# Position-bias tables read from 128 stored copies instead of turned by TensorE products

## The reference, cut to what matters

```python
REL_BUCKETS = 32; REL_MAX_EXACT = 16; REL_MAX_DIST = 128
def rel_bucket(dist):
    n = jnp.maximum(dist, 0)
    is_small = n < REL_MAX_EXACT
    large = REL_MAX_EXACT + (log(n / REL_MAX_EXACT) / log(REL_MAX_DIST / REL_MAX_EXACT) * 16).astype(int32)
    return where(is_small, n, minimum(large, REL_BUCKETS - 1))
...
x = x + 0.5 * swiglu(rmsnorm(x), w_ffn1_gate, w_ffn1_up, w_ffn1_down)      # first FFN
lg = einsum(q, k) * scale + tab[head, rel_bucket(t - s)]                     # mixer scores, s > t masked
```

## Time and profile before

| | |
|---|---|
| median of 3 runs | 1628.88 us (1625.75 to 1630.94) |
| profiled execution | 1628.55 us, its span 1627.2 us |
| granted TensorE clock, mean | 0.995 of full speed |
| TensorE (PE) busy | 1596.4 us, 98% of the span |
| VectorE (DVE) busy | 1036.8 us, 64% |
| ScalarE (ACT) busy | 868.8 us, 53% |
| GpSimd (POOL) busy | 126.7 us, 8% |
| moved by SP's queue q1 | 272.40 MB |
| moved by POOL's queue q0 | 6.37 MB |

### The profile page before, as it was taken

One profiled execution on the slowest core, in us unless ns is written; L12 is line 12 of the kernel. 1 busy time (PEld: TensorE's weight loads), 2 busy tenths in 40 slices (PEclk: granted clock), 3 DMA queues, 4 the chain that ended last, 5 costly groups with the idle time before them and its releaser, 6 DMA issues. The chain is left out here.

```text
span 1627.2 us, 26648 instructions
## 1 busy us (share of the span) xinstructions
PE 1596.4 (98%) x11270; PEld 1389.9 (85%) x11270; DVE 1036.8 (64%) x1430; ACT 868.8 (53%) x1272; POOL 126.7 (8%) x117
## 2 busy tenths in 40 slices
PE   7999999999999999999998999999999999999998
PEld 7888897888888898888997888888888898888886
DVE  5656564467665766567895686657766574686655
ACT  6555544446555655555755265555655555665553
POOL 0000020000000001000376001000020001001000
PEclk9999999999999999999999999999999999999999
DMA  7754554334555555654530155554655543445552
GB/s 283 286 180 174 183 167 155 105 104 179 204 199 181 181 206 182 207 181 156 185 105 4 55 207 207 184 204 156 234 180 193 195 156 129 153 170 204 199 181 78
DMA packets 40854, 280.46 MB, mean 172 GB/s; under 512 B 4794, under 2 KB 4794, under 8 KB 8864
## 3 DMA queue, kind: packets, MB, share of 16 engines
q1 hardware_dynamic: 39024, 272.40, 48.0%
q0 software_dynamic: 1712, 6.37, 1.1%
HBM read 277.14 MB, written 1.08 MB: 171 GB/s over the span
## 5 line engine op out<-in xcount | busy, mean ns | idle before, releaser
L233 PE MATMUL P<-xt,whi 128*128 128x512 f32 (+1 forms) x3264 | 729.6, 347 | 3.0 <-ACT whi L207 1.5
L233 PEld LDWEIGHTS P<-xt,whi 128*128 128x128 f32 x3264 | 561.1, 191 | 75.1 <-issue 9.1
L221 DVE TENSOR_TENSOR wlo<-raw,whi 128x2048 fp32r<-128x2048 f32 x245 | 560.1, 2290 | 66.5 <-PE P L233 53.6
L207 ACT ACTIVATE whi<-raw 128x2048 fp32r<-128x2048 f32 x245 | 467.4, 1909 | 117.9 <-PE P L233 97.0
L233 PE MATMUL P<-xt,wlo 128*128 128x256 f32 x2544 | 440.3, 283 | 0.0
L233 PEld LDWEIGHTS P<-xt,wlo 128*128 128x128 f32 x2544 | 387.5, 191 | 17.8
L607 DVE SCALAR_TENSOR_TENSOR AR<-P,AR 128x256 f32<-128x256 f32 x228 | 96.4, 423 | 240.4 <-ACT AR L600 240.4
L233 PE MATMUL P<-whi,hh 128*128 128x512 f32 x504 | 197.9, 393 | 0.0
L233 PE MATMUL P<-wlo,hh 128*128 128x512 f32 x504 | 196.8, 390 | 0.0
L233 PE MATMUL P<-whi,hl 128*128 128x512 f32 x504 | 196.1, 389 | 0.0
L600 ACT ACTIVATE AR<-P 128x256 f32<-128x256 f32 x228 | 85.8, 376 | 138.4 <-PE P L233 138.3
(11 more groups left out here) (226 smaller groups left out, 1026.7 us busy)
## 6 DMA issues: line engine op xcount, KB each, us to landing
raw<-ws SPq DMA_DIRECT2D x249, 1024.0 KB, 4.9
gb<-gains SPq DMA_DIRECT2D x14, 512.0 KB, 7.4
AR<-by_distance POOLq DMA_DIRECT2D x1, 3072.0 KB, 19.5
x<-x_in SPq DMA_DIRECT2D x2, 512.0 KB, 4.1
AR<-mem_in POOLq DMA_DIRECT2D x1, 1024.0 KB, 5.3
AR<-gains SPq DMA_DIRECT2D x2, 512.0 KB, 4.8
out<-x SPq DMA_DIRECT2D x2, 512.0 KB, 2.6
cs<-cst SPq DMA_DIRECT2D x1, 737.0 KB, 13.4
```

The costliest lines, as they stand in the source:

```text
L207: act.e.activation(k.whi[n % NHI][:, :], k.raw[u % NRAW][:, :], ACT.Copy).then_inc(*k.s_hi.inc(u))
L221: dve.e.tensor_tensor(k.wlo[n % NLO][:, :], k.raw[u % NRAW][:, :], k.whi[n % NHI][:, :].bitcast(F32), ALU.subtract).then_inc(*k.s_lo.inc(u))
L233: return pe.e.matmul(o, l, r, start=start, stop=stop, skip_group_check=True)
```

## The change

The values by distance are stored in DRAM 128 times per head: `by_distance` becomes 16 x 128 x 512, written by one DMA whose source is the same 16 partitions, each row repeated 128 times (4 MB). With 128 copies behind one another, a partition step of 511 values walks one copy further and one value back, so a single DMA reads the rows in the right order. POOL then issues two reads in place of one: `HANK` with 8 heads x 384 values, for the compressed keys only, and `BIAS` itself with 16 heads x 256 values. The products with `FLIP`, the copies from bank 7, the `FLIP` constant and its load go away. `CB` is made by two copies in ScalarE straight from `HANK`, at j = 8 instead of j = 10. The mixer's first scores wait for the DMA of `BIAS` instead of ScalarE's last copy.

```diff
-    k.dist = nc.dram_tensor("by_distance", (16, 512), F32).ap()
+    k.dist = nc.dram_tensor("by_distance", (16, 128, 512), F32).ap()
...
-    k.HANK = ar(k, 7168, 6144, "p (h c) -> p h c", h=16)
+    k.HANK = ar(k, 7168, 3072, "p (h c) -> p h c", h=8)
...
 def bias_tensor(k, pe, j):
-    if j >= 2:
-        r = j - 2
-        pe.wait_ge(*k.s_hank.after())
-        pe.wait_ge(*k.s_flip.after())
-        if r == 0:
-            pe.wait_ge(*k.s_ev.after("dist"))
-        else:
-            pe.wait_ge(*k.s_ea.after("bias", r - 1))
-        if r < 8:
-            last = mm(pe, k.P[7][:, :], k.FLIP, k.HANK[:, 2 * r:2 * r + 2, 0:256])
-        else:
-            for a in range(2):
-                c = 159 - 128 * a
-                last = mm(pe, k.P[7][:, a * 120:(a + 1) * 120], k.FLIP, k.HANK[:, 8:16, c:c + 225:16])
-        last.then_inc(*k.s_pe.inc("bias", r))
...
 def bias_scalar(k, act, j):
-    if j >= 2:
-        r = j - 2
-        act.wait_ge(*k.s_pe.after("bias", r))
-        if r < 8:
-            act.e.activation(k.BIAS[:, 2 * r:2 * r + 2, :], k.P[7][:, :].rearrange("p (h c) -> p h c", h=2),
-                             ACT.Copy).then_inc(*k.s_ea.inc("bias", r))
-        else:
-            act.e.activation(k.CB, k.P[7][:, 0:240].rearrange("p (a h n) -> p h a n", a=2, h=8),
-                             ACT.Copy).then_inc(*k.s_ea.inc("bias", r))
+    if j == 8:
+        act.wait_ge(*k.s_hank.after())
+        for a in range(2):
+            c = 159 - 128 * a
+            act.e.activation(k.CB[:, :, a, :], k.HANK[:, :, c:c + 225:16], ACT.Copy).then_inc(*k.s_ea.inc("cb", a))
...
 def bias_pool(k, pool):
     pool.wait_ge(*k.s_ev.after("dist"))
-    pool.e.dma_start(k.dist[:, :], k.VALS).then_inc(*k.s_dist.inc(by=16))
+    pool.e.dma_start(k.dist[:, :, :], k.VALS.unsqueeze(1).to_broadcast([16, 128, 512])).then_inc(*k.s_dist.inc(by=16))
     pool.wait_ge(*k.s_dist.after())
-    pool.e.dma_start(k.HANK, bass.AP(k.dist.tensor, 0, [[1, 128], [512, 16], [1, 384]])).then_inc(*k.s_hank.inc(by=16))
+    n, m = 511, 128 * 512
+    pool.e.dma_start(k.HANK, bass.AP(k.dist.tensor, 8 * m + 127, [[n, 128], [m, 8], [1, 384]])).then_inc(*k.s_hank.inc(by=16))
+    pool.e.dma_start(k.BIAS, bass.AP(k.dist.tensor, 127, [[n, 128], [m, 16], [1, 256]])).then_inc(*k.s_bias.inc(by=16))
...
     if step == 1:
         dve.wait_ge(*k.s_pe.after("cl"))
-        dve.wait_ge(*k.s_ea.after("bias", 8))
+        dve.wait_ge(*k.s_ea.after("cb", 1))
...
-            return [k.s_dup[0].after(), k.s_dup[1].after(), k.s_po.after("dup", 0), k.s_ea.after("bias", 7)] + (
+            return [k.s_dup[0].after(), k.s_dup[1].after(), k.s_po.after("dup", 0), k.s_bias.after()] + (
...
 def mixer_pool(k, pool):
-    pool.wait_ge(*k.s_ea.after("bias", 8))
+    pool.wait_ge(*k.s_ea.after("cb", 1))
...
-    pool.e.dma_start(k.FLIP, k.cst[:, C_FLIP:C_FLIP + 128]).then_inc(*k.s_flip.inc(by=16))
```

More of the change, by code:

```diff
@@ L25 @@
 C_ID, C_TRI, C_KEEP, C_CEN, C_BLK = 0, 128, 256, 384, 512
-C_MLT, C_MLE, C_LEV, C_SCAN, C_I64, C_ONES, C_FLIP = 642, 706, 770, 1154, 1410, 1474, 1602
-C_END = C_FLIP
-C_SEL = C_FLIP + 128
+C_MLT, C_MLE, C_LEV, C_SCAN, C_I64, C_ONES, C_END = 642, 706, 770, 1154, 1410, 1474, 1602
+C_SEL = C_END
 C_ALL = C_SEL + 72 + 768
@@ L146, in tiles_and_signals @@
     k.s_gn = [sig("gn0"), sig("gn1")]
-    k.s_id, k.s_vec, k.s_cst, k.s_flip, k.s_base, k.s_rel = (
-        sig(n) for n in ("id", "vec", "cst", "flip", "base", "rel"))
-    k.s_dist, k.s_hank, k.s_w2, k.s_mem = (sig(n) for n in ("dist", "hank", "w2", "mem"))
+    k.s_id, k.s_vec, k.s_cst, k.s_base, k.s_rel = (
+        sig(n) for n in ("id", "vec", "cst", "base", "rel"))
+    k.s_dist, k.s_bias, k.s_hank, k.s_w2, k.s_mem = (sig(n) for n in ("dist", "bias", "hank", "w2", "mem"))
     k.s_dup = [sig(f"dup{i}") for i in range(8)]
@@ L939, in mixer_tiles @@
     k.VALS = k.AR[0:16, 13840:14352]
-    k.FLIP = k.AR[:, 14352:14480]
     k.QA = ar(k, 7168, 1024, "p (j t) -> p j t", j=4)
@@ L3218, in constants @@
     c[:, C_ONES:C_ONES + 128] = 1
-    c[:, C_FLIP:C_FLIP + 128] = np.eye(128)[::-1]
     for j in range(6):
```

## The result

The changed kernel takes 1640.83 us (median of 7 runs, 1638.34 to 1649.99) against 1628.88 us before (7 runs now, 1625.75 to 1632.83); the ratio is 1.0083, 95% interval 1.0054 to 1.0112. It is slower by 12 us where I forecast 8 us faster, and it lies outside my range, which ended at 1628.0 us. The profiled execution took 1639.22 us. It is rival C, the slow write that starves the weights, in its mechanism and its time; the two numbers that it was worked out from were a write of 64 us and 115 GB/s for the weights, and here they are 48.3 us and 93 GB/s.

A forecast was written before the change was run, and what follows sets the result against it. TensorE, busy 98% of the span, was taken as the bound; 8.2 us saved, with 0 for DMA traffic, gave 1628.55 - 8.2 = 1620.3 us, forecast as a 1620.6 us median, range 1618.0 to 1628.0 us.

The forecast's parts named there:

- rival C: First FFN: a 64 us write leaves the weights 115 GB/s, TensorE loses 19.7 us, time 1640 us; chance 8%.
- What bounds the kernel: First FFN: TensorE never idles, busy all 74.00 us from 106 to 180 us, so a `FLIP` product costs 0.86 us.
- The saving of 6.0 + 2.2 = 8.2 us: TensorE, first FFN: seven `FLIP` products give 6.0 us, the last products and a wait at its end 2.21 us.
- Rival A: End of first FFN: VectorE's and ScalarE's chain takes back 2.2 us, leaving 6.0 us gained, 1622.9 us; chance 15%.
- ScalarE, the waits for `HANK` and `BIAS`: First FFN and mixer: removed copies count nothing; both transfers arrive 45 us before 180 us even at worst.
- The duration of the write: POOL's queue from 47 us: the 4.19 MB write takes 30 us, from the earlier read's 161 GB/s and somewhat more.
- bounds of 17 and 64 us: Write time from the small write's row: 17 us by engine time over all 16 engines, 64 us by bytes over time.
- the reading as bytes over time: Small write's row: 33 KB in 0.5 us, 66 GB/s, which gives 64 us for the 4.19 MB write.
- So I take 0 for it: Foreign traffic's cost to TensorE in the first FFN: supply of 184 against 190 GB/s loses 1.6 us, taken by slack.
- The limit of about 10.5 us from issue to landing: Weight loads in the first FFN: landing times up to about 10.5 us do not reach TensorE.
- 5.6 us of slack: Weights' chain to TensorE: missed supply absorbed before TensorE loses time, the landing limit of 10.5 less 4.9 us undisturbed.
- The rule of the Trainium skill: DMA write: partitions 0 to 15 reach four of 16 ports, 104 GB/s, so the write would take 40 us.

The follow-up runs named there:

- e1_one_copy: Changed kernel with one stored copy of the values (32 KB) instead of 128, its tables in reverse row order: 1620.33 us, ratio 0.9939.
- e4: e1_one_copy plus a 4.19 MB scratch write to DRAM out of 128 SBUF partitions, each row 16 times: 1621.35 us, ratio 0.994.
- e5: e1_one_copy plus a 4.19 MB scratch write to DRAM out of 16 neighbouring SBUF partitions, each row 128 times: 1640.03 us, ratio 1.006.
- e7: As e5, but the 16 source partitions are 0, 8, 16, ... 120 instead of 0 to 15: 1621.56 us, one run.
- e3: Changed kernel with 24 copies (0.79 MB) instead of 128, and 24 reads, one per head and table, instead of two: 1622.45 us, ratio 0.9945.
- e6: Changed kernel with a distance between heads in DRAM of 260 KB instead of 256 KB: 1643.96 us, one run.
- e10: Changed kernel with the same write of 128 copies issued by ScalarE on its own queue instead of by POOL: 1640.66 us, one run.
- e11: Changed kernel with the write cut into eight writes of 16 copies, some 16.6 us apart, and CB made at j = 9: 1620.19 us, ratio 0.9954.
- e9: As e5, but the scratch write comes out of partitions 0 to 31, each row 64 times: 1624.67 us, one run.
- e2: Changed kernel with the values written to DRAM once and the 128 copies made by one DRAM-to-DRAM transfer: 1618.09 us, ratio 0.9926.

## Why the prediction was wrong

- What bounds the kernel: right. TensorE is full in this stage, and a `FLIP` product costs 0.86 us of it.
- The saving of 6.0 + 2.2 = 8.2 us: right. e1_one_copy ends the FFN 8.1 us earlier and takes 1620.33 us, against the forecast of 1620.6. Rival A, a loss at the end of the FFN, falls with it: the second addition is on time there, and the first follows the split as foreseen.
- ScalarE, the waits for `HANK` and `BIAS`: right. `HANK` was read 10.2 us after 96.0 us, long before j = 8.
- The duration of the write: my 30 us was too short. 48.3 us lay inside the bounds of 17 and 64 us. I took a value near the read of the earlier trace rows; that row is a transfer to 128 partitions, and e4 and e5 show that this was the difference that mattered, 21.9 against 45.2 us. Of the small write, the reading as bytes over time was the better guide, not the one as engine time.
- "So I take 0 for it": this is the step that failed, the term for what the foreign traffic does to TensorE. It took the supply of 184 GB/s that the weights keep beside a fast read as their supply beside a slow write. In the changed kernel they got 0.01 MB from 48 to 60 us, and 4.46 MB from 48 to 96 us, 93 GB/s. Put at 0, the term measured 20.1 us: 15.7 us of waits and 4.4 us of low clock. The limit of about 10.5 us from issue to landing was a little low: a load of 12.2 us (e7) cost TensorE nothing and one of 12.8 us (e3) 0.2 us. In the changed kernel, e5, e6 and e10 the loads that waits of TensorE go back to took 17.2 to 23.0 us, and each wait was 11.0 to 12.8 us shorter than its load: 23.0 us gave 10.26, 17.2 us gave 5.46. The loads of 23.6 and 27.1 us were issued while the first was still out and made no wait of their own.
- Rival C had the mechanism, and I gave it 8% because "two ends have to hold at once". They are not independent: a slow source makes the write long and starves the weights by the same cause. With the measured 48.3 us and 93 GB/s its formula gives 48.3 x 97 / 190 = 24.7 us missed, less 5.6 us of slack, 19.1 us, so from e1_one_copy's 1620.3 us it comes to 1639.4 us, against 1640.8 measured. That is partly luck. C's own inputs, 64 us and 115 GB/s, miss in opposite directions and give nearly the same 25.3 us. And the low clock, 4.4 us of the loss, was not in the formula, while TensorE waited 15.7 us for 24.7 us missed: the slack was 9 us and not 5.6, and the two errors nearly cancel.
- The rule of the Trainium skill (SBUF — State Buffer, "Door 1: The DMA port swizzle") that I set beside the sum gave an estimate of 40 us for the write, nearer to 48.3 us than my own 30. I named the chance that a slow source also holds back the weights, and left it out of the sum.

## What to carry to other kernels

A transfer's price for the others on the same DMA engines is how long at a stretch it holds them, not its bytes (e4 and e5 move the same) and not the total (e11 holds them for longer in all and costs nothing): look at busy share and GB/s side by side, and be wary of a large transfer whose one end lies in few neighbouring partitions. If many copies of a small tile are needed, write it once and copy it in DRAM, or cut the copying into pieces shorter than the slack of the stream beside it. Before costing a background transfer at nothing, compare the longest landing that the stream's consumers tolerate with the worst landing, not with an average rate; and when two bad ends have one cause, their chance is that of the cause.

## What the runs showed of the hardware that I had not expected

- The two queues do not share engine time evenly at the start of a large transfer. In the changed kernel the weights moved nothing from 48.5 to 63.8 us. The first line is POOL's queue in that gap; the other two are both queues from 64 to 84 us, in the middle of the write, when the weights have 154 GB/s beside it:

```profile
q0 software_dynamic: 360, 1.47, 92.4%
```

```profile
q0 software_dynamic: 440, 1.80, 63.3%
q1 hardware_dynamic: 420, 3.08, 36.5%
```

  From 84 to 92 us they fell back to 0.17 MB, 22 GB/s, and the load issued at 79.8 us took 17.2 us.
- By the times of the packets in the traces, the gap ended in all the slow writes in one piece when the other queue had moved about the same amount. It lasted 15.3 us and 1.47 MB in the changed kernel, 14.4 us and 1.46 MB in e5, 14.7 us and 1.48 MB in e6, and in e10, where the write goes by another queue in packets of half the size, 14.7 us and 1.45 MB. Where the same bytes come out of partitions eight apart (e7), it was 1.4 MB again and half as long, about 7 us:

```profile
q0 software_dynamic: 341, 1.40, 97.4%
```

  This line is POOL's queue from 47.5 to 54.5 us. Fast transfers open such a gap too, of 4 to 6 us: 1.25 MB in e9, 1.6 MB in e4 and in the read of the kernel before, 2.1 MB in e2. A piece of 0.5 MB (e11) is over in 5 to 6 us, before so much has moved, and the load behind it took 8 to 9 us; behind the 0.79 MB of e3 it took 11.2 us. So the slow source does not make the gap; it stretches it, from 4 to 7 us, which the weights' slack covers, to 15 us. No run was made to vary this amount, and why it is what it is stays open.
- TensorE's clock went down during a wait of 10 us and during one of 5.5 us, and cost 2.4 and 2.0 us afterwards, 4.4 us on top of the 15.7 us of the waits themselves.
- The changed kernel's runs spread by 0.7% (1638.3 to 1650.0 us), those of e1_one_copy by 0.4%. The two longest runs, 1649.99 and 1649.11 us, have the lowest mean granted clocks, 0.982 and 0.987, against 0.989 to 0.991 in the others, which would fit longer waits of TensorE; only one of the seven has a trace, so this was not shown.
